# The sample's output tile in two matmuls a piece: high and low rows side by side as stationary columns

## The chip, the cores and the metric

The kernel runs on one core of one Trainium2 chip. The time is the device time in microseconds of one launch on that core; several launches are timed and their median is taken. A separate profiled launch gives the trace that the rows below come from.

## The reference, cut to what matters

One layer of a streaming encoder for two groups of requests: a prompt of 1024 tokens and a sample of 32 tokens that continue a running stream. Both share all weights.

```python
def rms_norm(x, gain):
    xf = x.astype(jnp.float32)
    y = xf * lax.rsqrt(jnp.mean(xf * xf, axis=-1, keepdims=True) + NORM_EPS)
    return (y * gain.astype(jnp.float32)).astype(x.dtype)
...
    h = rms_norm(x, norm_pre[l])
    p = h @ w_in[l]                       # 2048 -> 7168 columns, split into q, k, v, gates of three head groups
    mixed = gated_concat(oa, ga, ob, gb, oc, gc)   # attention outputs times silu(gate), 2048 wide
    y = x + rms_norm(mixed @ w_out[l], norm_post[l])
```

The change touches only the last line, `mixed @ w_out` with its norm, and of it only the 32 rows of the sample. Everything is float32.

## The kernel before, in words

**Numbers in two parts.** TensorE works on a reduced float32 format (F32R). To keep float32's precision, each operand is split into a high part (the value rounded to that format) and a low part (what is left). A product is then three matmuls into the same PSUM bank: high times high, high times low and low times high. The fourth, low times low, is left out.

**Stages.** The normed activations lie in SBUF as `act_hi` and `act_lo`, features on the partitions (16 blocks `k` of 128) and 1056 tokens along the row: 1024 of the prompt and then 32 of the sample. `project` streams `w_in` through a ring of four pieces and makes q, k, v and gates, with the attention of all heads laid out between the matmuls by a hand-made plan (`pe_plan`, `act_plan`, `dve_plan`, `sp_plan`). The gated attention output goes to a scratch in DRAM and comes back into `act_lo`, from where ScalarE (ACT) makes `act_hi` and VectorE (DVE) turns `act_lo` into the low part.

**The output stage** (`out_mm`, from L962 on) is the one at stake. Here the activations are the stationary operand (128 token columns of one block `k`) and `w_out` is the moving one (a piece of 128 features by 512 output columns). Token tiles are numbered 0 to 7 for the prompt and 8 (`TT`) for the sample. The stage runs over eight **chunks**: chunks 0 to 3 are the four column pieces for token tiles 0 to 3, chunks 4 to 7 the same four column pieces for token tiles 4, 5, 6, 7 and 8 (`TOKSETS`, `CHUNKS`). A chunk goes over 16 positions `pos` (one weight piece each), and at each position over its tiles `j`, three matmuls each (L972, L973, L974). So a position has 12 matmuls in chunks 0 to 3 and 15 in chunks 4 to 7, of which the last three are the sample's. The sample's stationary operand is also 128 columns wide: 32 columns of its own and 96 of what lies behind them (the next block's first tokens; behind the last block 96 zeroed columns), whose results are never read.

In the last chunk the last four positions are taken tile by tile, so that the tiles end one after the other.

**Banks.** Tile number `s` (counted over all chunks) accumulates in PSUM bank `s % 8`. At `pos` 0 PE waits until the tile eight before it has left its bank (`y_out`, L966). In chunk 5 tile `j` = 3 waits for the first tile of chunk 4, and `j` = 4 for the second.

**The weight ring.** SP loads piece `pos` into one of four slots when PE has ended position `pos - 4` (`piece_used`, L651); ACT copies it to `w_hi` (L1155), DVE subtracts (`w_lo`, L1322), and PE waits for that (`lo_made`).

**What ACT and DVE do with a finished tile.** PE signals `y_done`. ACT's `squares` (L1241) reads the bank, writes squares to `y` and sums them along the row (an ACTIVATE and a read of the accumulator); DVE's `with_gain` (L1497) then multiplies the bank by the post gain into `y` and signals `y_out`. Both engines work strictly in the order of their programs: the first tile of a chunk at `pos` 14, then ACT's and DVE's part of the weight piece that follows, then the other tiles, then the next piece's part. In the last chunk each tile is followed on DVE by `variance` and by the previous tile's `finish_late` (four small instructions and two of 1024 columns at L1528), then SP stores.

**Chunk 4 also ends the first half.** DVE's `finish` (L1518) scales tiles 0 to 3 and adds the residual that SP has loaded in halves (L720), POOL stores each tile (L1604), and ACT waits for all four stores (`y_stored`) before its first `squares` of chunk 4, since `y` is used again.

Of the kernel before, what the change touches and what calls it, by code (L numbers as in the profile page):

```python
# [7 lines left out]
F32, F32R, BF16 = mybir.dt.float32, mybir.dt.float32r, mybir.dt.bfloat16  # L8
ALU, ACT, AX = mybir.AluOpType, mybir.ActivationFunctionType, mybir.AxisListType

P = 128
D = 2048
KT = D // P
SEQ, DEC, PAST = 1024, 32, 512
TOK = SEQ + DEC
# [20 lines left out]
PIECE = 512  # L36
RING = 4
TT = SEQ // P
# [150 lines left out]
for u in range(NU):  # L189
    if NEW_KV[u]:  # L190
        at = {n: 12 * TILE_OF[n, u] + 0.6 for n in "kv"}
# [125 lines left out]
TOKSETS = ((0, 1, 2, 3), (4, 5, 6, 7, 8))  # L317
NCH = D // PIECE
# [4 lines left out]
TILES_BEFORE = [sum(len(TOKSETS[g]) for g, _ in CHUNKS[:c]) for c in range(len(CHUNKS) + 1)]  # L323


def build(nc, x_prompt, x_sample, cache_a_k, cache_a_v, cache_b_k, cache_b_v, cache_c_k, cache_c_v,
# [3 lines left out]
    with ctx:  # L330
        ORIGIN, FLOATS = 16512, 53060
        ctx.enter_context(nc.sbuf_tensor("whole", [P, FLOATS], F32))
        at = [0]

        def place(name, shape, dt, floats, offset=None):

            if offset is None:
                offset = at[0]
                at[0] += floats
                assert at[0] <= FLOATS, at[0]  # L340
            return nc.alloc_sbuf_tensor_at(name, shape, dt, offset=ORIGIN + 4 * offset)

        def sem(name):
            return ctx.enter_context(nc.semaphore(name))

        ACT_N = KT * TOK
        act_hi_t = place("act_hi", [P, ACT_N + P - DEC], F32R, ACT_N + P - DEC)
        act_lo_t = place("act_lo", [P, ACT_N + P - DEC], F32R, ACT_N + P - DEC)
        act_hi = act_hi_t[:, 0:ACT_N].rearrange("p (k t) -> p k t", k=KT)
        act_lo = act_lo_t[:, 0:ACT_N].rearrange("p (k t) -> p k t", k=KT)  # L350

        res_hi = place("res_hi", [P, KT, TOK], F32, 0, 0)
        res_lo = place("res_lo", [P, KT, TOK], F32, 0, ACT_N + P - DEC)
        ring0 = at[0]
        w_raw = place("w_raw", [P, RING, PIECE], F32, RING * PIECE)
        w_lo = place("w_lo", [P, RING, PIECE], F32R, 0, ring0)
        w_hi = place("w_hi", [P, RING, PIECE], F32R, RING * PIECE)
# [32 lines left out]
        y = arena[:, 0:5 * D].rearrange("p (t c) -> p t c", t=5)  # L390
        post_gain = [arena[:, 5 * D + 512 * i:5 * D + 512 * i + 512] for i in (0, 1)]
# [12 lines left out]
        ps = ctx.enter_context(nc.psum_tensor("ps", [P, 8 * 512], F32))  # L404

        def bank(b, n=512, r=P, c=0):
            return ps[0:r, 512 * b + c:512 * b + c + n]
# [24 lines left out]
        consts, zeroed = sem("consts"), sem("zeroed")  # L432
# [16 lines left out]
        mixed_in = [sem(f"mixed_in{i}") for i in range(len(MIXED_LOADS))]  # L449
        last_stored = sem("last_stored")  # L450
        mx_hi, mx_lo = sem("mx_hi"), sem("mx_lo")
        post_in = [sem("post_in0"), sem("post_in1")]
        y_done, y_sq, y_out = sem("y_done"), sem("y_sq"), sem("y_out")
        yv_sum, yv_var, yv_std, yv_rstd = (sem(n) for n in ("yv_sum", "yv_var", "yv_std", "yv_rstd"))
# [49 lines left out]
        def rows_of(t):  # L504
            return P if t < TT else DEC
# [242 lines left out]
        def _(pe):  # L748
            mm = nc.tensor.matmul
# [212 lines left out]
            def out_mm(c, pos, j):  # L962
                g, n = CHUNKS[c]
                k, s = KORD[pos], TILES_BEFORE[c] + j
                slot = (P3 + KT * c + pos) % RING
                if pos == 0 and s >= 8:  # L966
                    pe.wait_ge(y_out, s - 7)
                elif pos == 0 and s < 3:
                    pe.wait_ge(proj_out, 3 * (TILES - 1) + s + 1)
                t0 = TOK * k + P * TOKSETS[g][j]  # L970
                th, tl = act_hi_t[:, t0:t0 + P], act_lo_t[:, t0:t0 + P]
                mm(bank(s % 8), th, w_hi[:, slot, :], start=(pos == 0), stop=False)  # L972
                mm(bank(s % 8), th, w_lo[:, slot, :], start=False, stop=False)  # L973
                last = mm(bank(s % 8), tl, w_hi[:, slot, :], start=False, stop=(pos == KT - 1))  # L974
                if pos == KT - 1:
                    last.then_inc(y_done, 1)
                elif j == len(TOKSETS[g]) - 1:
                    last.then_inc(piece_used, 1)
# [8 lines left out]
            for _, what, u, n in pe_plan():  # L987
# [35 lines left out]
                elif what == "turn_cache":  # L1023
# [3 lines left out]
                    for b in range(cache_blocks(u)):  # L1027
                        last = nc.tensor.transpose(bank(zb, P, P, P * b), kc[:, b, :], ident[:, :])
# [11 lines left out]
            for pos in range(LEAD):  # L1040
                out_mm(0, pos, 3)

            for c, (g, n) in enumerate(CHUNKS):
                tiles = len(TOKSETS[g])
# [15 lines left out]
        def _(act):  # L1060
            fn = nc.scalar.activation
# [95 lines left out]
            def mixed_hi(pos):  # L1157
                k = KORD[pos]
                act.wait_ge(mixed_in[LOAD_OF[k]], 16)
                fn(act_hi[:, k, :], act_lo[:, k, :].bitcast(F32), ACT.Copy).then_inc(mx_hi, 1)  # L1160

            for _, what, u, n in act_plan():
# [35 lines left out]
                elif what == "keep":  # L1198
# [3 lines left out]
                    for c, a, b in RUNS["b"][n]:  # L1202
                        last = fn(oT[:, a:b], bank(O_BANK, b - a, P, c), ACT.Copy)
# [32 lines left out]
            def squares(c, j):  # L1236
                g, n = CHUNKS[c]
                s, tt = TILES_BEFORE[c] + j, TOKSETS[g][j]
                rows = rows_of(tt)
                act.wait_ge(y_done, s + 1)  # L1240
                fn(y[0:rows, j, PIECE * n:PIECE * n + PIECE], bank(s % 8, 512, rows), ACT.Square,  # L1241
                   accum_out=ssq_y[0:rows, 4 * tt + n:4 * tt + n + 1]).then_inc(y_sq, 1)

            def following_high(c, pos):
                if pos + RING < KT:
                    out_high(c, pos + RING)
                elif c + 1 < len(CHUNKS):
                    out_high(c + 1, pos + RING - KT)
# [3 lines left out]
            for c, (g, n) in enumerate(CHUNKS):  # L1252
                tiles = len(TOKSETS[g])
                last_chunk = c + 1 == len(CHUNKS)
                for pos in range(KT - 1):
                    if pos == KT - 2 and not last_chunk:
                        if c == NCH:
                            act.wait_ge(y_stored, 16 * len(TOKSETS[0]))
                        squares(c, 0)
                    following_high(c, pos)  # L1260
                    if c == 0 and pos + 4 < KT:
                        mixed_hi(pos + 4)
                    if c == NCH and pos == 0:
                        for tt in TOKSETS[0]:
                            std_of(tt)
                for j in range(0 if last_chunk else 1, tiles):
                    squares(c, j)
                    if last_chunk and j:
                        std_of(TOKSETS[1][j - 1])
                if last_chunk:  # L1270
                    std_of(TOKSETS[1][-1])
                following_high(c, KT - 1)
# [3 lines left out]
        def _(dve):  # L1276
            v = nc.vector

            v.memset(act_hi_t[:, ACT_N:].bitcast(F32), 0.0)
            v.memset(act_lo_t[:, ACT_N:].bitcast(F32), 0.0).then_inc(zeroed, 1)  # L1280
            v.memset(qbd[:, :], 0.0).then_inc(zeroed, 1)

            dve.wait_ge(rel_in, 16)
# [49 lines left out]
            def tile_out(T, g):  # L1333
                what, u = TILE[T]
                dst = {"k": kT[KV[u] % 2], "v": tmp, "q": qT, "g": gT}[what]
                d = dst[:, GN * g:GN * g + GN]
                if what == "g" and g == 0:
                    if u:
                        dve.wait_ge(mix_stored, STORED[u - 1])
                dve.wait_ge(proj_done, 3 * T + g + 1)  # L1340
                if what != "q":
                    v.tensor_copy(d, bank(g, GN)).then_inc(proj_out, 1)  # L1342
                    return
                if g == 2 and UNITS[u][0] == "a":
                    if u == 0:
                        dve.wait_ge(zeroed, 2)
                    for h in range(2):
                        hp = slice(DH * h, DH * h + DH)
                        c = 512 * g + SEQ - GN * g
                        v.tensor_scalar(qbd[hp, DEC * h:DEC * h + DEC], ps[hp, c:c + DEC], SCALE, None, ALU.mult)  # L1350
                v.tensor_scalar(d, bank(g, GN), SCALE, None, ALU.mult).then_inc(proj_out, 1)
# [111 lines left out]
            for _, what, u, n in dve_plan():  # L1463
# [8 lines left out]
                elif what == "cap":  # L1472
                    dve.wait_ge(e_ready, step_no(u, n))
                    w = sum(piece[2] for piece in A_STEPS[n])
                    s = stick[(STEP0[u] + n) % 2]
# [15 lines left out]
            def with_gain(c, j):  # L1491
                g, n = CHUNKS[c]
                s = TILES_BEFORE[c] + j
                rows = rows_of(TOKSETS[g][j])
                dve.wait_ge(post_in[c % 2], 16 * (c // 2 + 1))
                dve.wait_ge(y_sq, s + 1)
                v.tensor_tensor(y[0:rows, j, PIECE * n:PIECE * n + PIECE], bank(s % 8, 512, rows),  # L1497
                                post_gain[c % 2][0:rows, :], ALU.mult).then_inc(y_out, 1)

            def variance(tt):  # L1500
                vy = var_y[0:rows_of(tt), tt:tt + 1]
# [32 lines left out]
            for c, (g, n) in enumerate(CHUNKS):  # L1534
                tiles = len(TOKSETS[g])
# [113 lines left out]
```

## Time and profile before

| What | Value |
|---|---|
| median of 3 runs | 2200.77 us (2198.38 to 2201.91) |
| the profiled execution's own time | 2200.49 us |
| its span, first to last instruction | 2198.7 us |
| mean granted TensorE clock | 0.991 |
| PE busy | 2140.4 us (97%), 13970 matmuls |
| DVE busy | 1000.1 us (45%) |
| ACT busy | 768.2 us (35%) |
| output stage, first to last matmul | 1772.05 to 2182.91 us, 1728 matmuls |

Busy times of an engine are summed over the span. Matmuls are pipelined: one takes 0.39 us from its start to its end, but the next starts about 0.23 us after it, so that what a matmul costs is the distance of two starts and not its duration. Idle time of an engine that nothing waits for costs nothing. Times are counted from the first instruction.

### The profile page before, as it was taken

To read this page: it belongs to the slowest core of one execution; us is meant where nothing else is said; L and a number is where in the kernel's file an instruction comes from. 1 tells how busy PE (TensorE), PEld (TensorE's weight loads), DVE (VectorE), ACT (ScalarE), POOL (GpSimd) and SP (SyncE) were. 2 spreads that over 40 slices of the span, in tenths; PEclk is the share of its full clock that TensorE was granted. 3 is DMA by queue.
4 is the path that set the end of the run, shared out by engine and by line. 5 is a ranking of instruction groups with operands and counts; after the bars stand their busy time and mean duration, and the time that the engine had idled before them with its cause. 6 is when DMAs were issued, how large, how long until landed. Compare 5 with 4: busy or idle time off the path is not lost.

```text
span 2198.7 us, 32401 instructions
## 1 busy us (share of the span) xinstructions
PE 2140.4 (97%) x13970; PEld 1936.4 (88%) x13970; DVE 1000.1 (45%) x1923; ACT 768.2 (35%) x1340; POOL 9.4 (0%) x28
## 2 busy tenths in 40 slices
PE   4999999999999999999999999999999999999996
PEld 4998988989888898999999999999999978887885
DVE  6345565655555565433324242444334463334224
ACT  5234344443434444332323232333233453222221
POOL 0000000000000000000000000000000000000000
PEclk8999999999999999999999999999999999999998
DMA  6211111111111111212111111222122353337423
GB/s 236 71 55 44 54 39 54 54 53 54 39 52 46 49 58 35 64 39 69 34 60 45 52 55 37 62 49 54 40 58 49 118 166 101 99 102 239 140 81 125
DMA packets 211813, 161.18 MB, mean 73 GB/s; under 512 B 60040, under 2 KB 186264, under 8 KB 209912
## 3 DMA queue, kind: packets, MB, share of 16 engines
q1 hardware_dynamic: 210504, 151.13, 23.0%
q0 software_dynamic: 1168, 7.99, 1.0%
q8 instruction: 110, 1.80, 0.3%
q14 instruction: 31, 0.25, 0.0%
HBM read 132.72 MB, written 29.57 MB: 74 GB/s over the span
## 4 chain that ended last, share of the span: by engine, by line
PE 91%; DVE 5%; ACT 2%; DMA 1%; issue 0%; SPq 0%; DVEq 0%; ACTq 0%
PE ps L768 19%; PE ps L769 18%; PE ps L770 18%; PE ps L974 6%; PE ps L973 6%; PE ps L972 6%; PE ps L857 3%; PE ps L951 3%; PE ps L824 3%; PE ps L922 3%; PE ps L884 2%; PE ps L869 2%; DVE arena L1394 1%; PE ps L959 1%; DMA arena<-in_x_prompt_dram 1%; DVE arena L1388 1%
## 5 line engine op out<-in xcount | busy, mean ns | idle before, releaser
L768 PE MATMUL ps<-act_hi,w_hi 128*128 128x352 f32 x2688 | 889.1, 331 | 3.9 <-DVE arena L1342 3.2
L770 PE MATMUL ps<-act_hi,w_lo 128*128 128x352 f32 x2688 | 869.1, 323 | 0.0
L769 PE MATMUL ps<-act_lo,w_hi 128*128 128x352 f32 x2688 | 869.1, 323 | 0.0
L768 PEld LDWEIGHTS ps<-act_hi,w_hi 128*128 128x128 f32 x2688 | 507.2, 189 | 33.7 <-issue 28.7
L769 PEld LDWEIGHTS ps<-act_lo,w_hi 128*128 128x128 f32 x2688 | 507.7, 189 | 0.0
L770 PEld LDWEIGHTS ps<-act_hi,w_lo 128*128 128x128 f32 x2688 | 507.1, 189 | 0.0
L1322 DVE TENSOR_TENSOR w_lo<-w_raw,w_hi 128x512 fp32r<-128x512 f32 x352 | 241.5, 687 | 332.9 <-ACT w_hi L1155 244.1
L972 PE MATMUL ps<-w_hi,act_hi 128*128 128x512 f32 x576 | 227.0, 394 | 5.8 <-DVE w_lo L1322 3.0
L974 PE MATMUL ps<-w_hi,act_lo 128*128 128x512 f32 x576 | 229.5, 398 | 0.0
L973 PE MATMUL ps<-w_lo,act_hi 128*128 128x512 f32 x576 | 228.6, 397 | 0.0
L1155 ACT ACTIVATE w_hi<-w_raw 128x512 fp32r<-128x512 f32 x128 | 80.8, 631 | 276.6 <-DMA w_raw<-in_w_out_dram 276.6
L1079 ACT ACTIVATE w_hi<-w_raw 128x512 fp32r<-128x512 f32 x224 | 138.9, 621 | 102.8 <-DMA w_raw<-in_w_in_dram 102.8
L1149 ACT ACTIVATE arena<-arena,small 128x257 f32<-128x257 f32 (+4 forms) x180 | 101.0, 565 | 137.0 <-DVE small L1424 137.0
L972 PEld LDWEIGHTS ps<-w_hi,act_hi 128*128 128x128 f32 x576 | 109.8, 191 | 33.2 <-DVE w_lo L1322 3.5
L1182 ACT ACTIVATE arena<-arena 128x1024 f32<-128x1024 f32 (+1 forms) x60 | 61.1, 1018 | 208.8 <-DVE arena L1402 208.8
L1477 DVE TENSOR_SCALAR arena<-arena 128x1024 f32<-128x1024 f32 (+1 forms) x60 | 40.1, 669 | 202.0 <-ACT arena L1174 202.0
L973 PEld LDWEIGHTS ps<-w_lo,act_hi 128*128 128x128 f32 x576 | 108.5, 188 | 26.1
L974 PEld LDWEIGHTS ps<-w_hi,act_lo 128*128 128x128 f32 x576 | 108.6, 188 | 24.5
L1342 DVE COPY arena<-ps 128x352 f32<-128x352 f32 x120 | 62.0, 522 | 138.9 <-PE ps L770 138.4
L1388 DVE TENSOR_TENSOR arena<-ps,arena 128x1024 f32<-128x1024 f32 (+1 forms) x60 | 70.4, 1174 | 68.8 <-ACT arena L1178 68.8
L1115 ACT ACTIVATE arena<-ps 128x1024 f32<-128x1024 f32 x54 | 55.3, 1025 | 107.4 <-PE ps L869 107.4
L1424 DVE CUSTOM_DVE_ANT_0 arena<-ps,arena 128x640 f32<-128x640 f32 (+5 forms) x72 | 44.0, 661 | 83.6 <-PE ps L857 83.6
(132 smaller groups left out, 1785.4 us busy)
## 6 DMA issues: line engine op xcount, KB each, us to landing
w_raw<-in_w_in_dram SPq DMA_DIRECT2D x176, 256.0 KB, 2.9
w_raw<-in_w_out_dram SPq DMA_DIRECT2D x128, 256.0 KB, 3.0
w_raw<-in_w_in_dram SPq DMA_DIRECT2D x96, 128.0 KB, 2.4
out_dram<-arena SPq DMA_DIRECT2D x20, 512.0 KB, 3.2
arena<-in_x_prompt_dram SPq DMA_DIRECT2D x8, 1024.0 KB, 5.8
mixed_scratch<-arena SPq DMA_DIRECT2D x10, 528.0 KB, 4.1
act_lo<-mixed_scratch SPq DMA_DIRECT2D x2, 2112.0 KB, 10.3
arena<-in_x_prompt_dram SPq DMA_DIRECT2D x8, 512.0 KB, 5.8
```

Of the source, the lines that this page charges most:

```text
L768: mm(bank(g, GN), wh, ah, start=(k == 0), stop=False)
L769: mm(bank(g, GN), wh, al, start=False, stop=False)
L770: last = mm(bank(g, GN), wl, ah, start=False, stop=(k == KT - 1))
L824: last = mm(bank(zb + h, w, P, c), qT[hp, P * m:P * m + P], keys[hp, k0:k0 + w], start=(c == 0), stop=True, skip_group_check=True)
L972: mm(bank(s % 8), th, w_hi[:, slot, :], start=(pos == 0), stop=False)
L973: mm(bank(s % 8), th, w_lo[:, slot, :], start=False, stop=False)
L974: last = mm(bank(s % 8), tl, w_hi[:, slot, :], start=False, stop=(pos == KT - 1))
L1079: fn(w_hi[:, q, :], w_raw[:, q, :], ACT.Copy).then_inc(hi_made, 1)
L1149: fn(s, s, ACT.Exp, bias=neg_max[0:rows_of(m), t:t + 1], scale=-1.0, accum_out=row_sum[0:rows_of(m), t:t + 1]).then_inc(p_exp, 1)
L1155: fn(w_hi[:, pc % RING, :], w_raw[:, pc % RING, :], ACT.Copy).then_inc(hi_made, 1)
L1322: v.tensor_tensor(w_lo[:, slot, :], w_raw[:, slot, :], w_hi[:, slot, :].bitcast(F32), ALU.subtract).then_inc(lo_made, 1)
L1388: v.tensor_tensor(both, z, both, ALU.max).then_inc(sp_ready, 1)
```

## The change

For the sample's tile (`tt == TT`) the low columns are laid beside the high ones, and the pair is one stationary operand: columns 0 to 31 of each block of `act_hi` get the sample's high part and columns 32 to 63 its low part. The rest of the 128 columns keeps what token tile 0 had there. Two matmuls a piece (with `w_hi` and with `w_lo`) give the high rows' sum in PSUM partitions 0 to 31 and the low rows' sum in partitions 32 to 63, low times low included. Both are added at the end.

- ACT makes the pair with two copies (`pair`) behind the last `squares` of chunk 3, when token tile 0 isn't needed any more; PE waits for them (`paired`) before the sample's first matmul of chunk 4.
- For each sample tile ACT first copies the low rows from PSUM into `y` (`low_moved`), DVE adds the bank's high rows to them (`joined`), ACT squares the sum from `y`, and DVE's gain takes it from `y` too.
- The padding columns behind `act_hi` and `act_lo`, and the two memsets that zeroed them, go.

```diff
-        act_hi_t = place("act_hi", [P, ACT_N + P - DEC], F32R, ACT_N + P - DEC)
-        act_lo_t = place("act_lo", [P, ACT_N + P - DEC], F32R, ACT_N + P - DEC)
...
+        act_hi = place("act_hi", [P, KT, TOK], F32R, ACT_N)
+        act_lo = place("act_lo", [P, KT, TOK], F32R, ACT_N)
+
+        pair_rows = act_hi[:, :, 0:P]
...
-                t0 = TOK * k + P * TOKSETS[g][j]
-                th, tl = act_hi_t[:, t0:t0 + P], act_lo_t[:, t0:t0 + P]
-                mm(bank(s % 8), th, w_hi[:, slot, :], start=(pos == 0), stop=False)
-                mm(bank(s % 8), th, w_lo[:, slot, :], start=False, stop=False)
-                last = mm(bank(s % 8), tl, w_hi[:, slot, :], start=False, stop=(pos == KT - 1))
+                tt = TOKSETS[g][j]
+                out, wh, wl = bank(s % 8), w_hi[:, slot, :], w_lo[:, slot, :]
+                if tt == TT:
+
+                    if c == NCH and pos == 0:
+                        pe.wait_ge(paired, 2)
+                    mm(out, pair_rows[:, k, :], wh, start=(pos == 0), stop=False)
+                    last = mm(out, pair_rows[:, k, :], wl, start=False, stop=(pos == KT - 1))
+                else:
+                    th, tl = act_hi[:, k, P * tt:P * tt + P], act_lo[:, k, P * tt:P * tt + P]
+                    mm(out, th, wh, start=(pos == 0), stop=False)
+                    mm(out, th, wl, start=False, stop=False)
+                    last = mm(out, tl, wh, start=False, stop=(pos == KT - 1))
...
+                out, src = y[0:rows, j, PIECE * n:PIECE * n + PIECE], bank(s % 8, 512, rows)
                 act.wait_ge(y_done, s + 1)
-                fn(y[0:rows, j, PIECE * n:PIECE * n + PIECE], bank(s % 8, 512, rows), ACT.Square,
+                if tt == TT:
+
+                    fn(out, ps[DEC:2 * DEC, 512 * (s % 8):512 * (s % 8) + 512], ACT.Copy).then_inc(low_moved, 1)
+                    act.wait_ge(joined, n + 1)
+                    out, src = src, out
+                fn(out, src, ACT.Square,
                    accum_out=ssq_y[0:rows, 4 * tt + n:4 * tt + n + 1]).then_inc(y_sq, 1)
+
+            def pair(src, at):
+
+                act.wait_ge(y_done, TILES_BEFORE[NCH])
+                fn(act_hi[:, :, at:at + DEC], src[:, :, SEQ:TOK].bitcast(F32), ACT.Copy).then_inc(paired, 1)
...
                     squares(c, j)
+                    if c == NCH - 1 and j == tiles - 1:
+                        pair(act_hi, 0)
+                        pair(act_lo, DEC)
...
-            v.memset(act_hi_t[:, ACT_N:].bitcast(F32), 0.0)
-            v.memset(act_lo_t[:, ACT_N:].bitcast(F32), 0.0).then_inc(zeroed, 1)
...
+                o = y[0:rows, j, PIECE * n:PIECE * n + PIECE]
+                src = bank(s % 8, 512, rows)
+                if rows == DEC:
+                    dve.wait_ge(low_moved, n + 1)
+                    v.tensor_tensor(o, src, o, ALU.add).then_inc(joined, 1)
+                    src = o
                 dve.wait_ge(y_sq, s + 1)
-                v.tensor_tensor(y[0:rows, j, PIECE * n:PIECE * n + PIECE], bank(s % 8, 512, rows),
-                                post_gain[c % 2][0:rows, :], ALU.mult).then_inc(y_out, 1)
+                v.tensor_tensor(o, src, post_gain[c % 2][0:rows, :], ALU.mult).then_inc(y_out, 1)
```

## Rows read from the trace of the kernel before

**Rows 1.** The page: busy time, and the engines of the chain that ended last

```profile
PE 2140.4 (97%) x13970; PEld 1936.4 (88%) x13970; DVE 1000.1 (45%) x1923; ACT 768.2 (35%) x1340; POOL 9.4 (0%) x28
...
PE 91%; DVE 5%; ACT 2%; DMA 1%; issue 0%; SPq 0%; DVEq 0%; ACTq 0%
```

**Rows 2.** Busy by stretch: chunks 4, 5, 6 and 7 to position 11; columns named

```profile
core 0: us, PE busy (x) PEld busy (x) DVE busy (x) ACT busy (x) POOL busy (x), PEclk, DMA share, GB/s
1955.52:2011.34 55.82, 55.82 (x241) 45.24 (x240) 26.08 (x51) 13.61 (x27) 2.17 (x4) 1.00 0.67 226
2011.34:2068.16 56.82, 56.30 (x241) 45.08 (x240) 14.80 (x22) 13.92 (x29) 0.00 (x0) 1.00 0.49 158
2068.16:2123.99 55.83, 55.83 (x241) 45.24 (x240) 14.20 (x21) 13.06 (x27) 0.00 (x0) 1.00 0.26 80
2123.99:2165.83 41.84, 41.84 (x181) 33.95 (x180) 10.73 (x16) 9.87 (x21) 0.00 (x0) 1.00 0.26 82
```

**Rows 3.** Timeline at the start of chunk 4: start, duration, engine, line, instruction

```profile
1953.30 0.63 ACT L1155 ACTIVATE w_hi<-w_raw 128x512 fp32r<-128x512 f32 x1 [2.31 <-DMA w_raw<-in_w_out_dram]
1953.84 0.58 ACT L1241 ACTIVATE arena<-ps 128x512 f32<-128x512 f32 x1
...
1958.09 0.21 ACT L1241 ACTIVATION_READ_ACCUMULATOR arena<-ps 128x1 f32 x1
...
1955.52 0.39 PE L972 MATMUL ps<-w_hi,act_hi 128*128 128x512 f32 x1
...
1958.29 0.39 PE L972 MATMUL ps<-w_hi,act_hi 128*128 128x512 f32 x1
```

**Rows 4.** Timeline around the start of chunk 5, and DMA in the 28 us before

```profile
1984.00:2012.00 28.00, 28.00 (x122) 22.71 (x121) 15.22 (x27) 5.05 (x8) 2.17 (x4) 1.00 0.93 325
...
1987.10 0.33 SPq L651 DMA_DIRECT2D w_raw<-in_w_out_dram  x1
...
2007.33 0.53 POOL L1604 DMA_DIRECT2D out_dram<-arena  x1 [8.15 <-DVE arena L1518]
...
2012.01 0.60 ACT L1241 ACTIVATE arena<-ps 128x512 f32<-128x512 f32 x1 [2.60 <-DMA out_dram<-arena]
...
2013.55 0.50 PE L972 MATMUL ps<-w_hi,act_hi 128*128 128x512 f32 x1
...
2015.02 0.50 PE L972 MATMUL ps<-w_hi,act_hi 128*128 128x512 f32 x1 [0.51 <-DVE arena L1497]
```

**Rows 5.** Timeline at the start of chunk 6, ACT and DVE

```profile
2070.14 0.57 ACT L1241 ACTIVATE arena<-ps 32x512 f32<-32x512 f32 x1
...
2069.21 2.47 DVE L1497 TENSOR_TENSOR arena<-ps,arena 128x512 f32<-128x512 f32 x4
2072.11 0.69 DVE L1322 TENSOR_TENSOR w_lo<-w_raw,w_hi 128x512 fp32r<-128x512 f32 x1 [0.43 <-ACT w_hi L1155]
```

**Rows 6.** Timeline of the tail: the last chunk's tiles on ACT, DVE and PE

```profile
2174.93 0.60 ACT L1241 ACTIVATE arena<-ps 128x512 f32<-128x512 f32 x1 [2.11 <-PE ps L974]
...
2175.72 0.69 DVE L1497 TENSOR_TENSOR arena<-ps,arena 128x512 f32<-128x512 f32 x1 [1.86 <-ACT arena L1241]
...
2182.91 0.39 PE L974 MATMUL ps<-w_hi,act_lo 128*128 128x512 f32 x1
...
2187.96 0.67 DVE L1497 TENSOR_TENSOR arena<-ps,arena 32x512 f32<-32x512 f32 x1
```

**Rows 7.** Timeline of PE behind two stalls, at 1786 and 2171 us

```profile
1786.30 0.51 PE L972 MATMUL ps<-w_hi,act_hi 128*128 128x512 f32 x1 [2.26 <-DVE act_lo L1460]
...
1787.40 0.63 PE L973 MATMUL ps<-w_lo,act_hi 128*128 128x512 f32 x1
...
1790.38 0.55 PE L974 MATMUL ps<-w_hi,act_lo 128*128 128x512 f32 x1
...
2171.12 0.51 PE L972 MATMUL ps<-w_hi,act_hi 128*128 128x512 f32 x1 [3.02 <-DVE w_lo L1322]
```

**Rows 8.** Timeline of DVE at the start of the kernel

```profile
6.76 0.22 DVE L1284 COPY arena<-arena 8x128 f32<-8x128 f32 x1 [5.53 <-DMA arena<-in_rel_bias_dram]
```

More of the change, by code:

```diff
@@ L346, in build @@
         ACT_N = KT * TOK
-        act_hi_t = place("act_hi", [P, ACT_N + P - DEC], F32R, ACT_N + P - DEC)
-        act_lo_t = place("act_lo", [P, ACT_N + P - DEC], F32R, ACT_N + P - DEC)
-        act_hi = act_hi_t[:, 0:ACT_N].rearrange("p (k t) -> p k t", k=KT)
-        act_lo = act_lo_t[:, 0:ACT_N].rearrange("p (k t) -> p k t", k=KT)
+        act_hi = place("act_hi", [P, KT, TOK], F32R, ACT_N)
+        act_lo = place("act_lo", [P, KT, TOK], F32R, ACT_N)
+        pair_rows = act_hi[:, :, 0:P]
         res_hi = place("res_hi", [P, KT, TOK], F32, 0, 0)
-        res_lo = place("res_lo", [P, KT, TOK], F32, 0, ACT_N + P - DEC)
+        res_lo = place("res_lo", [P, KT, TOK], F32, 0, ACT_N)
         ring0 = at[0]
@@ L451, in build @@
         mx_hi, mx_lo = sem("mx_hi"), sem("mx_lo")
+        paired, low_moved, joined = sem("paired"), sem("low_moved"), sem("joined")
         post_in = [sem("post_in0"), sem("post_in1")]
@@ L1345, in tile_out @@
                     if u == 0:
-                        dve.wait_ge(zeroed, 2)
+                        dve.wait_ge(zeroed, 1)
                     for h in range(2):
```

## The prediction

> **What bounds the kernel now.** I read the page first: PE is busy 97% of the span and makes 91% of the chain that ended last [rows 1]. So PE is the bound, and a matmul taken out counts wherever nothing else keeps PE waiting. The change lies in chunks 4 to 7, so next comes the busy time by stretch [rows 2]. Chunks 4 and 6 and chunk 7 up to position 11 have a full PE at full clock; chunk 5 holds 1 us more span than chunk 4 for the same 240 matmuls. The price of a matmul is the distance of two starts: chunk 6 takes 55.83 us for 240, so 0.2326 us each [rows 2]. Then I looked, on the timeline, for the places where PE stops or soon would. There are three.
>
> At the start of chunk 5 PE waits for its banks. The first tile's `squares` runs at 2012.01, after ACT idled for a store (`y_stored`); tile 3 starts at 2013.55 and tile 4 at 2015.02, the latter 0.51 us idle [rows 4]. DMA is nearly full there: a share of 0.93 and 325 GB/s over the last 28 us of chunk 4 [rows 4].
>
> At position 15 of chunk 7 PE idles 3.02 us until the last weight piece is made [rows 7]. That piece's slot comes free when position 11 ends, so this stall moves with PE and keeps its length.
>
> From 2175.72 on DVE, not PE, sets the end. Its gain of the last chunk's second tile follows ACT at 2175.72; the sample's gain runs only at 2187.96, though PE's last matmul starts at 2182.91 [rows 6]. In between DVE has no gap that PE could shorten.
>
> About 0.2% (4.4 us) is what a measurement of this kernel can tell from no change.
>
> **The change part by part.**
>
> *Matmuls removed.* One of three per position of the sample's tile: 16 in each of chunks 4, 5 and 6, 12 in chunk 7 before the tile-by-tile part, and 4 in that part. The last 4 (0.93 us) end the sample's tile sooner, but DVE reaches it some 5 us after PE is done [rows 6], so I count them at nothing. Were DVE quicker there, they would count in full.
>
> *The wide stationary operand.* It had 128 columns before and has 128 now, and the two remaining matmuls stream 512 columns as before. No cost.
>
> *The pair.* ACT makes it behind its last read of the accumulator, which starts at 1958.09. ACT starts the next instruction about 0.1 us after such a start, at 1958.19. The nearest row to a copy of 128 by 512 elements is the weight copy, 0.63 us long and 0.54 us from start to next start [rows 3]. Two end at 1958.19 + 0.54 + 0.63 = 1959.36. PE wants the sample's first matmul at 1958.29 [rows 3]. So PE stands for about 1.1 us, and the first matmuls behind a stall take 0.2 us more (0.50 long in place of 0.39 [rows 3, 4], and the second is late by as much): 1.3 us. The short runs of 32 columns could make the copies longer; twice as long would be 1.2 us more. Whether this counts at all depends on the next place.
>
> *The start of chunk 5.* Chunk 4 loses 16 matmuls, 3.72 us, less the 1.3: PE would be 2.4 us early. But tile 3 of chunk 5 needs the first tile's gain, and that needs ACT, which waits for the store issued at 2007.33 and landed at 2012.01 [rows 4]. The store ends a chain of residual loads, DVE `finish` and stores that runs through the crowded DMA. How far does it move? If it followed PE, by 2.4 us. If it hangs on the piece issued at 1987.10, when position 8 was done [rows 4], PE is then 9 x 0.2326 - 1.3 = 0.8 us early, and that is the most I see it gain. If DMA's bytes decide, nothing; and PE being 2.4 us ahead lets two thirds of one more 256 KB piece in before the store, 0.17 MB at 325 GB/s, or 0.6 us later. I take the middle of 0 and 0.8: the 13th matmul of chunk 5 (2015.02) starts 0.4 us earlier, with bounds of 0.6 later and 2.4 earlier. I choose so because DMA is at 0.93 [rows 4]. PE then stops about 2 us at tile 3, and this hides the 1.3 us of the pair: PE only arrives later at a wait that it would have had anyway. If that cover is gone, the pair costs its 1.3 us.
>
> *What counts behind it.* The sample's removed matmul of position 0 of chunk 5 and 15 more there, 16 in chunk 6, 12 in chunk 7: 44 x 0.2326 = 10.2 us.
>
> *ACT and DVE between chunks.* In place of one ACT square (start 2070.14) come a copy, DVE's add behind its third gain (about 2071.0, 0.7 us) and a square from `y`; ACT's next weight copy goes from about 2071.4 to 2072.4, near 1 us later, and with it the subtraction at 2072.11, done 2072.80 [rows 5]. PE needs that piece at position 3, 45 matmuls into chunk 6 (2068.16 + 10.47 = 2078.6). Of 5.8 us slack, 1 goes to ACT and 0.7 to three missing matmuls; 4.1 stay. Cost nothing. The second tile's gain, which PE's fifth tile waits for, ends about 2069.9 against PE's arrival at 2070.95 [rows 2, 5]; one missing matmul leaves 0.8. Also nothing.
>
> *The tail.* DVE meets the add where it met the gain, at 2187.96. ACT's copy is long done. The add moves everything on by about 0.67 us, then ACT squares, and DVE must wait for that: 0.79 us from a square's start to its gain's [rows 6], and some 0.05 for the signal. Then the gain, of the same shape as before. Square roots wait behind ACT's square but end under that gain. Added: 0.67 + 0.05 + 0.79 = 1.5 us, all on the chain. Bounds: 1.2 to 1.9.
>
> *The memsets.* They lie ahead of 5.5 us in which DVE waits for a load [rows 8]. Nothing.
>
> **The sum.** 0.4 + 10.2 - 1.5 = 9.1 us less. Against the profiled execution's own time (2200.49; its span and 1.8 us around it) that makes 2191.4. That execution lies 0.3 us under the median of the three, which I leave aside. Bounds of the boundary term alone: 2192.4 and 2189.4; runs of one kernel spread over 3.5 us. The forecast's own range is 2188.8 to 2193.5.
>
> **The rivals.**
>
> *The store follows PE.* Then the boundary gives 2.4 us, and the pair's 1.3 us are on the path: 2.4 + 10.2 - 1.5 = 11.1, 2189.4. For it: SP issues loads in step with PE. Against: the 0.93 share. 0.12.
>
> *The clock falls.* After the 2.26 us stall at 1786.30, with other gaps shortly before, the seven distances between the matmuls at 1787.40 and 1790.38 were 0.43 us in place of 0.23 [rows 7]: about 1.5 us lost. After 3.02 us at 2171.12 there is no such thing: the second tile ends in time for ACT at 2174.93 [rows 6]. The new stall of 2 us at chunk 5 could be either. With one fall, 2192.9; with a second at the pair, 2194.4. 0.12. By the Trainium skill ("TensorE: Matmul & The Clock Gate", "What's actually happening") an idle PE falls from 2.4 to 1.2 GHz and activity brings it back, which bears on this case; the stalls of this trace show both outcomes.
>
> *A matmul gives back less than its distance.* If the weight load or the issue of the neighbours set the pace, taking out every 15th would give less. Nothing in the rows says so: chunks of 12 and of 15 matmuls run at the same distance. If only 0.13 came back for each, 44 give 5.7 and the sum is 4.6: 2195.9. 0.04. The Trainium skill (same page, "Back-to-back issue gap") gives about 131 ns for each 512-column matmul in a sustained stream of load and matmul pairs. The trace disagrees, at 232.6 ns.
>
> *Slower: ACT's queue.* ACT stands in its own order while DVE adds, and the weight copy behind it comes late at each of three chunk starts. It decides from 4.1 us of delay (the slack above), after which each further microsecond stops PE. To end 0.2% slower, the three starts would have to lose 13.5 us, or 8.6 us of delay each. The rows give 1. 0.03, about 2206.
>
> *The change doesn't do what it says.* All 64 matmuls stay in effect, and the tail's 1.5 us comes on top: 2202. 0.02.
>
> **How the numbers follow.** The forecast has 0.67, the rest as above. The range has to leave out no more than 0.2: 2188.5 to 2195.0 holds forecast, early store and clock cases with the runs' spread. Faster by over 0.2% is below 2196.4: forecast, store, clock and over half of the fourth, 0.93. Within 0.2%: 0.02. Slower, the last two: 0.05.
>
> **What would show it.** PE has 64 matmuls fewer, and chunk 6 takes 224 x 0.2326 = 52.1 us. PE stands about 1.1 us before the sample's first matmul of chunk 4, released by ACT's copy. At the start of chunk 5 ACT still waits for the store and PE stops for about 2 us at tile 3; the 13th matmul lies at about 2014.6. At the end DVE has a 0.9 us gap between the add and the gain, and PE's last matmul starts some 7 us before the sample's gain. Wrong would be: no stop at chunk 5 (the store was not the bound), a distance of 0.43 behind it (the clock), or a pair that takes several microseconds.

## The result, and the profile after

The changed kernel takes 2177.53 us (median of 4 runs, 2175.65 to 2179.85), against 2201.34 for the kernel before on the same chip: a ratio of 0.9891, with a 95% interval of 0.9877 to 0.9905. That is 24 us less, where 9 were forecast. The profiled execution took 2175.65 us, with a span of 2173.8.

First come the page's busy times and its chain, to be read against [rows 1]. PE has 64 matmuls fewer, as it should; DVE's share of the chain grows from 5 to 7%.

```profile
span 2173.8 us, 32282 instructions
...
PE 2108.8 (97%) x13906; PEld 1909.4 (88%) x13906; DVE 1001.7 (46%) x1925; ACT 771.0 (35%) x1346; POOL 9.4 (0%) x28
...
PE 87%; DVE 7%; ACT 2%; DMA 2%; issue 1%; SPq 0%; DVEq 0%; POOL 0%; ACTq 0%; POOLq 0%
```

PE's busy time lost 31.6 us, which is too much for 64 matmuls: at 0.2326 us each they are worth 14.9. Next comes the busy time by stretch, for chunks 1, 4, 5 and 6 of the changed kernel (the last three answer to [rows 2]; columns as there), and after it chunk 1 of the kernel before.

```profile
1806.82:1851.19 44.37, 44.37 (x194) 36.14 (x192) 13.56 (x20) 12.42 (x24) 0.00 (x0) 1.00 0.32 101
1939.92:1992.74 52.82, 51.74 (x226) 41.89 (x224) 25.67 (x51) 14.43 (x29) 2.16 (x4) 1.00 0.66 230
1992.74:2047.96 55.22, 53.44 (x226) 43.14 (x225) 15.88 (x24) 14.32 (x30) 0.00 (x0) 0.97 0.52 170
2047.96:2099.37 51.41, 51.41 (x225) 42.15 (x224) 14.79 (x22) 13.72 (x27) 0.00 (x0) 1.00 0.27 87
```

```profile
1821.48:1866.16 44.68, 44.68 (x194) 36.19 (x192) 13.57 (x20) 12.43 (x24) 0.00 (x0) 1.00 0.33 100
```

Chunk 1 has the same 192 matmuls in both kernels, and the change does not touch them. Yet it takes 44.37 us in place of 44.68, with a full PE at full clock in both. The timeline shows the same one stage earlier: here is the first matmul of the output stage, of the kernel before and of the changed one.

```profile
1772.05 0.50 PE L972 MATMUL ps<-w_hi,act_hi 128*128 128x512 f32 x1
```

```profile
1758.85 0.50 PE L981 MATMUL ps<-w_hi,act_hi 128*128 128x512 f32 x1
```

So 13.2 of the span's 24.9 us are gained before any instruction that the diff edits on PE. What lies there is mostly the projection, with 8064 matmuls of 352 columns. Where two of them follow each other without a stop (some 7600 pairs in each trace), their starts were 161.29 ns apart on average and are now 159.38.

Now the timeline of the places that the forecast named, in the changed kernel. This is PE at the start of chunk 4:

```profile
1942.44 0.39 PE L983 MATMUL ps<-w_hi,act_lo 128*128 128x512 f32 x1
1943.91 0.47 PE L977 MATMUL ps<-w_hi,act_hi 128*128 128x512 f32 x1 [1.07 <-ACT act_hi L1262]
```

PE and ACT at the start of chunk 5 (against [rows 4]):

```profile
1995.35 0.60 ACT L1256 ACTIVATE arena<-ps 128x512 f32<-128x512 f32 x1 [2.87 <-DMA out_dram<-arena]
...
1996.88 0.68 PE L981 MATMUL ps<-w_hi,act_hi 128*128 128x512 f32 x1 [1.78 <-DVE arena L1524]
1997.36 0.63 PE L982 MATMUL ps<-w_lo,act_hi 128*128 128x512 f32 x1
```

The tail, with PE's last matmul, and DVE's add and gain of the sample's tile (against [rows 6]):

```profile
2161.53 0.67 DVE L1521 TENSOR_TENSOR arena<-ps,arena 32x512 f32<-32x512 f32 x1
2162.99 0.68 DVE L1524 TENSOR_TENSOR arena<-arena 32x512 f32<-32x512 f32 x1 [0.79 <-ACT ps L1256]
```

These went as forecast. PE stands 1.07 us for the pair (1.1 forecast). At chunk 5 ACT waits for the store, and PE stops for 1.78 us at tile 3. From the start of the add to that of the gain are 1.46 us (1.5 forecast). But behind the stop at chunk 5 the matmuls are 0.63 us long, and eight distances in a row are 0.43 us. The granted clock is 0.50 there, the 1.2 GHz level (1997.36 to 2000.30), and 0.97 over the whole chunk. The same happens to seven distances behind the stop of 2.85 us at the last weight piece (2143.15); before, there was no such fall at either place.

### The profile page after: what moved, and what is told of

It reads as the page before. It is cut to its first block, busy times and chain, and to the rows that moved or that the text cites. A ratio compares the mean times of both kernels' runs of the same rounds, so it can differ in the third digit from the quotient of the medians.

```text
span 2173.8 us, 32282 instructions
## 1 busy us (share of the span) xinstructions
PE 2108.8 (97%) x13906; PEld 1909.4 (88%) x13906; DVE 1001.7 (46%) x1925; ACT 771.0 (35%) x1346; POOL 9.4 (0%) x28
## 4 chain that ended last, share of the span: by engine, by line
PE 87%; DVE 7%; ACT 2%; DMA 2%; issue 1%; SPq 0%; DVEq 0%; POOL 0%; ACTq 0%; POOLq 0%
PE ps L769 18%; PE ps L770 18%; PE ps L771 18%; PE ps L981 5%; PE ps L983 5%; PE ps L982 5%; PE ps L858 3%; PE ps L952 3%; PE ps L825 3%; PE ps L923 3%; PE ps L885 2%; PE ps L870 2%; DVE arena L1415 2%; DMA arena<-in_x_prompt_dram 1%; DVE arena L1409 1%; PE ps L960 1%
## 5 line engine op out<-in xcount | busy, mean ns | idle before, releaser
L981 PE MATMUL ps<-w_hi,act_hi 128*128 128x512 f32 x512 | 203.6, 398 | 7.2 <-DVE w_lo L1343 2.8
L983 PE MATMUL ps<-w_hi,act_lo 128*128 128x512 f32 x512 | 202.0, 395 | 0.0
L982 PE MATMUL ps<-w_lo,act_hi 128*128 128x512 f32 x512 | 202.0, 394 | 0.0
L981 PEld LDWEIGHTS ps<-w_hi,act_hi 128*128 128x128 f32 x512 | 96.8, 189 | 30.7 <-DVE w_lo L1343 3.9
L983 PEld LDWEIGHTS ps<-w_hi,act_lo 128*128 128x128 f32 x512 | 97.1, 190 | 22.3
L982 PEld LDWEIGHTS ps<-w_lo,act_hi 128*128 128x128 f32 x512 | 97.2, 190 | 21.5
```

The lines of the kernel that those rows point to most:

```text
L981: mm(out, th, wh, start=(pos == 0), stop=False)
L982: mm(out, th, wl, start=False, stop=False)
L983: last = mm(out, tl, wh, start=False, stop=(pos == KT - 1))
```

## The experiments

What was open was the faster TensorE. The padding that went was 96 floats behind `act_hi` and 96 behind `act_lo`, so `act_lo` now lies 384 bytes and the weight ring 768 bytes earlier in each partition. Theory A is that these addresses set the distance of matmuls all over the kernel. Rival B is that something else of the change does it.

**Pair with the padding kept (e1).**

```diff
-        act_hi = place("act_hi", [P, KT, TOK], F32R, ACT_N)
-        act_lo = place("act_lo", [P, KT, TOK], F32R, ACT_N)
+        act_hi = place("act_hi", [P, KT, TOK], F32R, ACT_N + 96)
+        act_lo = place("act_lo", [P, KT, TOK], F32R, ACT_N + 96)
```

> The changed kernel, but with the 96 spare columns kept behind act_hi and behind act_lo, so that act_lo, the weight ring and all behind them lie at the addresses of the kernel before. Theory A (addresses: every matmul of the kernel starts a little sooner after the last because act_lo and the weight ring moved): the distance of the 352-column matmuls is back at about 161.2 ns and that of the 512-column ones at 232.6, and the time is before less the 9 to 11 us that the step-by-step sum gave, about 2191. Rival B (something else that came with the change, such as the shorter program or the pair, speeds TensorE): it stays at 2177.

Measured: 2193.51 against 2202.43, ratio 0.9959 (0.9946 to 0.9972). The 352-column matmuls are 161.32 ns apart again. Chunks 1 and 6:

```profile
1820.47:1865.15 44.68, 44.68 (x194) 36.20 (x192) 13.57 (x20) 12.42 (x24) 0.00 (x0) 1.00 0.31 100
2065.86:2117.94 52.08, 52.08 (x226) 42.21 (x225) 14.79 (x22) 13.71 (x27) 0.00 (x0) 1.00 0.27 86
```

With the old addresses PE is back at 44.68 us for chunk 1, and chunk 6 takes the 52.1 us of the forecast. The pair alone is worth 8.9 us (6 to 12 by the interval); the sum said 9.1. Rival B falls: the pair, the longer program of ACT and DVE and the missing memsets are all in this version.

**Three matmuls without the padding (e2).** The last block's sample matmuls use 32 stationary columns, since behind it there is no zeroed padding any more.

```diff
-        act_hi_t = place("act_hi", [P, ACT_N + P - DEC], F32R, ACT_N + P - DEC)
-        act_lo_t = place("act_lo", [P, ACT_N + P - DEC], F32R, ACT_N + P - DEC)
+        act_hi_t = place("act_hi", [P, ACT_N], F32R, ACT_N)
+        act_lo_t = place("act_lo", [P, ACT_N], F32R, ACT_N)
...
+                m = min(P, ACT_N - t0)
+                th, tl = act_hi_t[:, t0:t0 + m], act_lo_t[:, t0:t0 + m]
+                out = bank(s % 8, 512, m)
```

> The kernel before (three matmuls a piece for the sample's tile), but without the spare columns, so that all tensors lie at the changed kernel's addresses; the last block's sample matmuls use 32 stationary columns. Theory A: distances of about 159.4 and 231 ns, and 13 to 16 us less than before, 2185 to 2188. Rival B: 2201, as before.

Measured: 2185.97 against 2202.43, ratio 0.9925 (0.9912 to 0.9938), distance 159.39 ns. Chunk 1:

```profile
1806.52:1850.88 44.36, 44.36 (x193) 36.11 (x192) 13.57 (x20) 12.43 (x24) 0.00 (x0) 1.00 0.32 101
```

The addresses alone give 16.5 us with the old three matmuls. Most of it lies ahead of the output stage, whose first matmul starts at 1758.63 us in place of 1772.05. 8.9 and 16.5 make 25.4; the change measured 24. A is shown from both sides.

**Which tensor's place? (e3, e4)** e3 puts 192 spare floats behind `act_lo` only, so that the ring is back at its old place. e4 puts 96 behind `act_hi` and 32 behind `act_lo`. The edit of e3:

```diff
-        act_lo = place("act_lo", [P, KT, TOK], F32R, ACT_N)
+        act_lo = place("act_lo", [P, KT, TOK], F32R, ACT_N + 192)
```

> The changed kernel with 192 spare floats ahead of the weight ring only: w_raw, w_hi and all behind lie where they lay before, act_lo where it lies after the change. By theory A part of the 14 us comes back, as much as the ring's place is worth. If only an address modulo 256 bytes counts, the ring has not moved (768 bytes) and the time stays at 2177; if 512 bytes or more count, it is slower by several us.

> The changed kernel with act_lo 96 floats further (as before) and the weight ring 128 floats further (512 bytes). By theory A with act_lo as what counts: in the output stage the distance ahead of the low stationary operand is back at 233 ns for even blocks, and the time is several us over 2177, up to 2191. If act_lo's place is worth nothing: 2177.

Measured: e3 2177.59 (ratio 0.9881, 0.9864 to 0.9897), e4 2194.44 (0.996, 0.9947 to 0.9973). Chunk 1 of e3 and of e4:

```profile
1807.76:1852.12 44.36, 44.36 (x193) 36.11 (x192) 13.56 (x20) 12.42 (x24) 0.00 (x0) 1.00 0.31 101
```

```profile
1822.16:1866.85 44.69, 44.69 (x194) 36.20 (x193) 13.57 (x20) 12.42 (x24) 0.00 (x0) 1.00 0.32 100
```

The ring may move by 768 bytes for nothing (e3). With `act_lo` 384 bytes on, all of the gain is gone (e4, in which the ring moves by another 512).

**How must they lie? (e5, e6, e7)** e5 puts 32 floats (128 bytes) ahead of the ring, e6 puts them ahead of everything, and e7 puts 16 floats behind `act_hi` and 48 behind `act_lo`. The main line of e6:

```diff
-        at = [0]
+        at = [32]
```

> The changed kernel with the weight ring (and all behind it) 128 bytes further, act_hi and act_lo where they are. In the output stage of the changed kernel even blocks have distances of 226 to 231 ns and odd ones of 230 to 234. If what counts is how the stationary and the moving operand lie to each other modulo 256 bytes, the odd blocks are now the quick ones and the time may move either way by several us; if each operand's own place counts and the ring's does not matter, even blocks stay quick and the time is 2177.

> The changed kernel with act_hi, act_lo, the ring and all behind them 128 bytes further. If only how the tensors lie to each other counts, 2177 and the same table of distances. If the own place of each modulo 256 bytes counts, even and odd blocks change roles in the output stage; with equally many of both the time stays within a few us.

> The changed kernel with act_lo 64 bytes further and the ring 256 bytes further. If the effect has a grain of 128 bytes in act_lo's place against act_hi's, this is neither the quick place nor the slow one: between 2177 and 2194, and which end it is nearer to says how wide the quick place is.

Measured: e5 2176.48 (ratio 0.9878, 0.9852 to 0.9904), e6 2178.09 (0.9888, 0.9866 to 0.991), e7 2189.34 (0.9943, 0.9921 to 0.9966). The time says that e5 and e6 are as good as the change and that 64 bytes of `act_lo` cost 12 us. More is in the distances of chunks 1 to 3, worked out from the starts of the matmuls in each trace. An odd block of the activations lies 4224 bytes behind the even one, and so 128 bytes off it modulo 256. The columns are the mean distance in ns behind a matmul of high rows by `w_hi`, of high rows by `w_lo` and of low rows by `w_hi`, in even and in odd blocks; then comes the mean of the 352-column ones. Ahead stand the places of `act_hi`, `act_lo` and the ring modulo 256 bytes. The last row is of an experiment further down.

```
            places        hi,w_hi       hi,w_lo       lo,w_hi      352
                        even   odd    even   odd    even   odd
before    128   0 128   226.7 234.1   232.5 233.2   235.6 234.1   161.29
after     128 128 128   231.0 233.8   226.6 233.1   230.0 231.9   159.38
e4        128   0 128   226.7 234.1   232.6 233.3   235.6 234.1   161.37
e5        128 128   0   233.8 230.9   233.1 226.7   231.9 230.0   159.35
e6          0   0   0   231.0 233.9   226.6 233.1   230.0 231.9   159.43
e7        128 192 128   229.4 233.7   228.8 231.2   233.1 231.1   160.87
e9        alternating   228.0 228.0   226.0 226.0   228.5 228.5   159.61
```

e6 repeats the changed kernel's line though every place is another: only how the tensors lie to each other counts. In e5 even and odd change roles. So, for the 512-column matmuls, the next one starts after 226 to 231 ns on average where the moving weights and both stationary operands around it (its own and the next one's) lie alike modulo 256 bytes, and after about 232 to 236 where one of them lies 128 bytes off. In the kernel before, only one of six columns had that. e7, with `act_lo` 64 bytes off, fits neither group: its columns that this touches lie at 228.8 to 233.1. Its chunk 1 takes 44.39 us, as good as the changed kernel's, and what it loses it loses ahead of the output stage, whose first matmul starts at 1769.93 us.

The rule covers the smaller part of the effect: a chunk of the output stage gains 0.3 to 0.7 us by it, and there are eight. The 352-column matmuls of the projection, where most is gained, also want `act_lo` to lie like `act_hi`, but their distances don't follow this rule block by block. What in the chip does it is not shown.

The Trainium skill ("TensorE: Matmul & The Clock Gate", "Step-by-step: what each phase is for") says that TensorE reads the moving and the stationary operand through two ports, and that a weight load takes no read bandwidth from the running matmul. No run here shows the ports. The runs do show that the places of the two operands change the distance of matmuls by up to 4% (226.7 against 235.6 ns in the kernel before), and whether the two reads meet somewhere is open.

**The rule put to the test (e9).** Each slot of the ring gets 32 spare floats, and blocks 12 to 15 are taken in the order 13, 12, 15, 14, so that slot and block are even or odd together.

```diff
-KORD = [0, 1, 2, 3, 4, 5, 6, 7, 8, 12, 13, 14, 15, 9, 10, 11]
+KORD = [0, 1, 2, 3, 4, 5, 6, 7, 8, 13, 12, 15, 14, 9, 10, 11]
...
-        w_raw = place("w_raw", [P, RING, PIECE], F32, RING * PIECE)
+        w_raw = place("w_raw", [P, RING, PIECE + 32], F32, RING * (PIECE + 32))[:, :, 0:PIECE]
```

> The changed kernel with each slot of the weight ring 128 bytes further than a whole number of 256 bytes from the last (32 spare floats a slot), and the order of the blocks changed (13, 12, 15, 14 in place of 12 to 15) so that even blocks meet even slots. My rule from the tables so far: a 512-column matmul starts 226 to 231 ns after the last where the moving weights and both stationary operands around it lie alike modulo 256 bytes, and 232 to 234 ns where not. By it every block of the output stage is now quick: chunks 1 to 3 take about 44.0 us in place of 44.4, and the time is 3 us less, 2174. If the rule is wrong, the odd blocks keep their 233 ns. The projection has both kinds of slot now; its tables for either place of the ring had the same mean, so nothing should change there.

Measured: 2174.75 (ratio 0.9875, 0.9861 to 0.989). Chunks 1 and 6:

```profile
1809.09:1852.77 43.68, 43.68 (x193) 36.11 (x192) 13.57 (x20) 12.42 (x24) 0.00 (x0) 1.00 0.33 103
2050.69:2101.63 50.94, 50.94 (x226) 42.12 (x225) 14.79 (x22) 13.74 (x27) 0.00 (x0) 1.00 0.27 88
```

The last line of the table shows that odd blocks are now as quick as even ones, and chunk 1 falls from 44.37 to 43.68 us, more than the 44.0 expected. The projection, where nothing was expected, got slower: 159.61 ns apart in place of 159.38, and the first matmul of the output stage starts at 1760.41 us in place of 1758.85. By time alone the version can't be told from the changed kernel (the intervals overlap); by its chunks it can.

**The tail (e8).** DVE's add moves ahead of the residual work of the last-but-two tile. The edit's main lines:

```diff
                         variance(TOKSETS[1][j])
+                        if j == tiles - 2:
+                            join(c, tiles - 1)
```

> The changed kernel, with DVE's add of the last sample tile moved ahead of the residual work of the last-but-two tile, so that ACT's square runs beside that. My account of the tail (1.5 us added on DVE: 0.67 of add and 0.8 of waiting for the square) says that the wait ahead of the sample's last gain goes from 0.79 us to nothing and the span behind PE's last matmul is 0.8 us shorter; the time is 2176.7, which is less than a measurement can tell. If the wait was hidden elsewhere, the span behind the last matmul stays at 18.3 us.

Measured: 2177.54 (ratio 0.9886, 0.9864 to 0.9907). The timeline of its tail:

```profile
2160.53 0.67 DVE L1516 TENSOR_TENSOR arena<-ps,arena 32x512 f32<-32x512 f32 x1
...
2164.34 0.67 DVE L1530 TENSOR_TENSOR arena<-arena 32x512 f32<-32x512 f32 x1
```

The gain has no idle time before it now. The time behind PE's last matmul is 17.4 us (2175.1 less 2157.72), against 18.3 (2173.8 less 2155.50) in the changed kernel. That is 0.9 us less, where 0.8 was expected. The account of the tail holds; in the time of a run it doesn't show.

**The start of chunk 5 (e10).** Each tile's store of the first half gets a semaphore of its own, and ACT waits for it only when it comes to that tile:

```diff
-                        if c == NCH:
-                            act.wait_ge(y_stored, 16 * len(TOKSETS[0]))
...
+                if c == NCH and j < len(TOKSETS[0]):
+                    act.wait_ge(y_stored[j], 16)
```

> The changed kernel, in which ACT waits for the store of tile j of the first half only before it overwrites that tile's place in y, not for all four stores before the first. If these stores set the start of chunk 5, as my forecast said, PE's stop of 1.8 to 4 us at tile 3 of chunk 5 is gone, and with it the slow clock behind it: 3 to 5 us less, about 2173.5, unless weight pieces come late there by then. If something else holds PE, the stop stays.

Measured: 2173.08 (ratio 0.9868, 0.9851 to 0.9884). Chunk 5:

```profile
1993.72:2045.18 51.46, 51.46 (x225) 42.16 (x224) 15.79 (x24) 13.93 (x29) 0.00 (x0) 1.00 0.59 189
```

PE at tiles 3 and 4 of chunk 5, and ACT:

```profile
1995.58 0.39 PE L983 MATMUL ps<-w_hi,act_lo 128*128 128x512 f32 x1
1995.81 0.39 PE L981 MATMUL ps<-w_hi,act_hi 128*128 128x512 f32 x1
1996.04 0.39 PE L982 MATMUL ps<-w_lo,act_hi 128*128 128x512 f32 x1
1996.26 0.39 PE L983 MATMUL ps<-w_hi,act_lo 128*128 128x512 f32 x1
1996.49 0.39 PE L977 MATMUL ps<-w_hi,act_hi 128*128 128x512 f32 x1
...
1997.46 0.60 ACT L1258 ACTIVATE arena<-ps 128x512 f32<-128x512 f32 x1 [1.61 <-DMA out_dram<-arena]
```

PE doesn't stop in chunk 5, and the clock doesn't fall there (granted 1.00); ACT waits only before the fourth tile, where nobody waits for it. The last store was what held chunk 5.

**All three (e11), and what the pair is worth without cover (e12).** e11 joins e8, e9 and e10. e12 is e2 with the additions of e9 and e10, so it has three matmuls for the sample.

> The changed kernel with the early add of the tail (0.9 us less in its trace), the phased slots and the stores waited for apart. If the three add up: 0.9 + 3 + 4, about 2169.5. It would be the quickest version here.

> Three matmuls a piece for the sample's tile, as in the kernel before, but at the quick addresses, with the phased slots and the stores waited for apart (no pair, no add; the last block's sample matmuls use 32 stationary columns). Against the version with all three additions and the pair it tells what the pair is worth when no store hides it: 60 matmuls at 0.2275 us give 13.6, less 1.3 for making the pair and 0.7 for the tail's add: 11.7 us slower than that version's 2168.8, so 2180.5. If the pair's worth is again only about 9 us, as where the store held PE, it is 2178.

Measured: e11 2168.76 against 2202.69, ratio 0.9852 (0.9837 to 0.9867), with 2169.5 expected; e12 2180.98 against 2200.92, ratio 0.9906 (0.989 to 0.9923). e11 is the quickest version of all; its interval overlaps that of e10, so the order of these two is not shown by time. e12 against e11 gives 12.2 us by the medians (11.7 expected). The two were measured on different chips and each ratio is good to 3 or 4 us either way, so by time the 9 us of the other reading aren't excluded. The traces say more: chunk 4 takes 52.91 us in e11 and 56.00 in e12, chunk 5 51.06 and 54.75. With no store to hide them, the matmuls of chunk 4 count too.

## Why the prediction was wrong

**The bound and the price of a matmul** were right where addresses stay: 52.1 us for chunk 6 forecast, 52.08 in e1.

**The step that failed** is the one that took the padding away at the price of its two memsets: "They lie ahead of 5.5 us in which DVE waits for a load [rows 8]. Nothing." The memsets did cost nothing (PE's first instruction starts at 12.66 us before and at 12.68 after), but the padding is also an address. Without it `act_lo` lies like `act_hi` modulo 256 bytes, and the 9700 or so split matmuls start a little sooner on average: 16.5 us (e2), of which 13.4 lie ahead of the output stage. No term of the sum and no rival had this. The rival that a matmul gives back less than its distance took that distance for a constant of the shape. The trace of before already spoke against that: behind the matmul of high rows by `w_hi` the distance was 226.7 ns in even blocks and 234.1 in odd ones. I had averaged 240 matmuls.

**The pair** was right: PE stands 1.07 us for 1.1 forecast, and 1.04 to 1.18 in the profiles of all versions with the pair.

**The start of chunk 5** had the right mechanism (e10) and a size that one profile can't give. In e1, at the old addresses, PE stopped 3.46 us at tile 3. The 13th matmul came 61.0 us behind the start of chunk 4, where it had come 59.5 before: 1.5 us later, where I had 0.4 earlier and 0.6 later at worst. The store is all of it: counted from the start of chunk 4, ACT's wait for it ended at 58.15 us in place of 56.49, and tile 3 started 1.65 us later. But the store's landing moves from profile to profile. In the nine versions with the pair and the old wait it landed 55.4 to 58.9 us behind the start of chunk 4, earliest in the changed kernel itself, where the 13th matmul came 1.2 us earlier than before. Bounds of 0.6 and 2.4 around one profile's place were too narrow on the late side. Here is e1's PE and ACT:

```profile
2012.66 0.60 ACT L1256 ACTIVATE arena<-ps 128x512 f32<-128x512 f32 x1 [4.44 <-DMA out_dram<-arena]
...
2014.19 0.67 PE L981 MATMUL ps<-w_hi,act_hi 128*128 128x512 f32 x1 [3.46 <-DVE arena L1524]
2014.66 0.63 PE L982 MATMUL ps<-w_lo,act_hi 128*128 128x512 f32 x1
```

**The clock rival**, given 0.12, came true in most profiles: a fall behind the stop at chunk 5 in the changed kernel and in e1, and in six of the nine versions with the pair and the old wait. In e4, e6 and e8 PE stopped 1.32, 2.84 and 2.26 us and the granted clock stayed at 1.00, and in e10, where there is no stop, there is no fall at chunk 5. The price was right, about 1.5 us each. The Trainium skill ("TensorE: Matmul & The Clock Gate", "What's actually happening") says that an idle PE falls from 2.4 to 1.2 GHz. The traces agree in so far as every fall between the start of the output stage and PE's last matmul stands at a stop of PE; they also show stops of that length without one.

**The tail** was right: 1.46 us for 1.5, and the last four matmuls count for nothing. PE's last matmul lies 18.3 us ahead of the end in place of 15.8, which is 1.5 and the 0.93 of those four.

**The other rivals.** The store did not follow PE: 2.4 us earlier would be 54.1 us behind the start of chunk 4, and none of the nine landed before 55.4. No weight copy came late behind ACT's new wait at chunks 6 and 7. The change did what it says. A cost that nobody had listed shows in some profiles: while DMA is crowded, a weight piece comes late at the start of chunk 5 or inside chunk 4, and PE waits for `w_lo`, 0.33 us in e1 and 1.69 us in e9. Neither before nor the changed kernel has it.

That the parts at old addresses add up to 8.9 us for a forecast of 9.1 is partly luck. The profiled spans of before and e1 differ by 7.4 us, and 1.2 of these are gained in chunk 0, which the change doesn't touch. Here is chunk 0 before and in e1:

```profile
1772.05:1821.48 49.43, 47.17 (x203) 37.57 (x201) 30.61 (x33) 25.87 (x37) 1.81 (x3) 0.97 0.54 178
```

```profile
1772.22:1820.47 48.25, 45.71 (x203) 36.34 (x201) 30.32 (x33) 25.77 (x37) 1.81 (x3) 1.00 0.54 182
```

It is the clock: the fall of [rows 7] behind the stop at 1786.30 isn't there in e1, although PE stopped 2.54 us at the same place. So a fall was gained by chance in chunk 0 and another one lost at chunk 5.

## What to carry to other kernels

A change that takes away padding, or resizes a tensor ahead of others, moves every address behind it. For a kernel bound by TensorE, compare the distance of matmuls that the change doesn't touch before crediting the change itself, and separate the two with a version that keeps the addresses. When pricing a matmul from a mean distance, split the mean by address first. And where a wait on a counter covers several transfers, look whether the first user needs only the first one.

## What was not expected of the hardware

In this kernel the distance of equal matmuls depends on how the operands lie to each other modulo 256 bytes: 226 to 231 ns against 232 to 236 for 512 columns, 159.4 against 161.3 on average for 352. Over this kernel that is 16.5 us by 384 bytes of one tensor's place (e2), and 64 bytes off already cost 12 us, nearly all of it in the projection (e7). Moving everything together by 128 bytes changes nothing (e6). In the projection I know only the mean, not the rule. And the granted clock fell behind some stops of PE of 1.8 to 4.0 us and not behind others of up to 3.0 us: behind the same stop in chunk 0, it fell in the profile of before and did not in e1's.
